# Prompt attention in four column groups of 32 keys, with transposes on VectorE and maxima gathered on GpSimd

## The reference

```python
scale = (D_NOPE + D_ROPE) ** -0.5
k_chunk = k_pos // CHUNK
def block(args):
    qb, pb = args
    s = jnp.einsum('bqhd,bkhd->bhqk', qb, k, preferred_element_type=F32) * scale
    mask = k_chunk[None, :] <= (pb // CHUNK)[:, None]
    p = jax.nn.softmax(jnp.where(mask[None, None], s, -jnp.inf), axis=-1)
    return jnp.einsum('bhqk,bkhd->bqhd', p.astype(v.dtype), v)
```

## Time and profile before

| what | us |
|---|---|
| median of 3 runs | 3896.78 (3894.89 to 3902.31) |
| the profiled execution, its own time | 3894.74 |
| its span, first to last instruction | 3893.0 |
| TensorE busy in the span | 3681.9 (95%) |
| VectorE, ScalarE busy | 1713.1 (44%), 1260.6 (32%) |
| GpSimd busy | 167.9 (4%) |
| the attention stage (first load to last store) | 1467.3 to 2128.9 |

### The profile page before, as it was taken

How to read it: one execution, slowest core, us unless ns; L and a number is a source line. 1 busy time by engine, 2 the same in 40 slices (tenths; PEclk the granted TensorE clock), 3 DMA queues, 4 the chain that set the end, 5 groups by cost and what they waited for, 6 DMA issues and landing times. The chain is left out here.

```text
span 3893.0 us, 64007 instructions
## 1 busy us (share of the span) xinstructions
PE 3681.9 (95%) x25552; PEld 2615.4 (67%) x25552; DVE 1713.1 (44%) x4404; ACT 1260.6 (32%) x3117; POOL 167.9 (4%) x193
## 2 busy tenths in 40 slices
PE   6999999979998888999999998999999999899998
PEld 3777777758887545666665445677767767677775
DVE  2443434445554244655555222221121122499996
ACT  1111111125553225655554001222122111355553
POOL 0000000011110000000000000000000000000100
PEclk8999999989999998999999999999999999899999
DMA  7111111143210011000002664111111111434433
GB/s 289 48 52 60 46 46 46 44 110 109 79 53 28 21 50 36 24 22 17 12 14 77 214 219 141 71 65 59 70 61 57 70 70 65 179 114 149 153 129 117
DMA packets 123523, 319.68 MB, mean 82 GB/s; under 512 B 38744, under 2 KB 57096, under 8 KB 118088
## 3 DMA queue, kind: packets, MB, share of 16 engines
q1 hardware_dynamic: 120568, 290.58, 20.5%
q0 software_dynamic: 2768, 26.47, 2.4%
HBM read 207.26 MB, written 109.74 MB: 81 GB/s over the span
## 5 line engine op out<-in xcount | busy, mean ns | idle before, releaser
L2373 PE MATMUL e_p<-e_hT,w_ahead 128*128 128x128 f32 x3264 | 410.7, 276 | 3.6 <-DMA shared<-w_in_o 3.6
L2373 PEld LDWEIGHTS e_p<-e_hT,w_ahead 128*128 128x128 f32 x3264 | 389.3, 193 | 11.7 <-issue 11.7
L535 PEld LDWEIGHTS a_p<-a_hT,w_even 128*128 128x128 f32 x3264 | 368.9, 193 | 9.4 <-issue 7.7
L535 PE MATMUL a_p<-a_hT,w_even 128*128 128x128 f32 x3264 | 369.1, 276 | 1.3 <-DVE a_hT L318 1.3
L550 PE MATMUL a_p<-w_even,a_hT 128*128 128x512 f32 (+2 forms) x1024 | 369.8, 522 | 0.0
L550 PEld LDWEIGHTS a_p<-w_even,a_hT 128*128 128x128 f32 x1024 | 193.9, 191 | 164.5 <-issue 115.4
L1696 DVE TENSOR_REDUCE q_mx<-q_sps 128x1 f32<-128x512 f32 (+4 forms) x320 | 181.5, 583 | 215.7 <-PE q_sps L1537 214.7
L2220 PE MATMUL c_b<-shared,c_oc 128*128 128x512 f32 x512 | 225.7, 601 | 11.6 <-DMA c_oc<-scr_ob 11.6
L2765 PE MATMUL h_b<-h_w,h_oT 128*128 128x512 f32 x512 | 236.6, 596 | 0.0
L2324 ACT ACTIVATE e_r<-e_p 128x512 f32<-128x512 f32 x66 | 39.4, 597 | 518.5 <-PE e_p L2379 299.0
L1625 ACT ACTIVATE q_P<-q_sps,q_mx 128x512 f32<-128x512 f32 (+4 forms) x320 | 190.7, 603 | 20.3 <-DVE q_mx L1701 15.5
(11 more groups left out here) (461 smaller groups left out, 5790.8 us busy)
## 6 DMA issues: line engine op xcount, KB each, us to landing
scr_qkg<-e_r SPq DMA_DIRECT2D x68, 512.0 KB, 2.6
h_rq<-scr_qkg SPq DMA_DIRECT2D x17, 2048.0 KB, 10.4
scr_iz<-e_r SPq DMA_DIRECT2D x34, 512.0 KB, 2.6
scr_qkv<-a_cv SPq DMA_DIRECT2D x17, 768.0 KB, 3.2
d_sc<-scr_qkv SPq DMA_DIRECT2D x17, 768.0 KB, 4.2
wa<-w_ada SPq DMA_DIRECT2D x8, 1536.0 KB, 16.2
w_ahead<-w_ada POOLq DMA_DIRECT2D x8, 1536.0 KB, 7.8
w_ahead<-w_in_o POOLq DMA_DIRECT2D x6, 2048.0 KB, 10.6
```

The costliest lines, as they stand in the source:

```text
L535: mm = pe.matmul(bank[g][:, (c % 4) * P:(c % 4 + 1) * P], w[:, k, c * P:(c + 1) * P], hT[:, p, k, :], start=k == 0, stop=k == KD - 1)
L2373: mm = pe.matmul(bank[n % 4][:, c * P:(c + 1) * P], w[k][:, a:a + P], hT[:, p, k, :], start=k == 0, stop=k == KD - 1)
```

## The change

The scores get another layout. A head's queries of one tile are cut in 4 blocks of 32 (`u`), and the keys of each tile in 4 groups of 32 (`i`). One matmul has 32 queries as stationary operand and all keys of one group (32·kt of them) as moving operand, and it writes the 32 partitions of column group `i`; so four matmuls fill 128 partitions, 16 make a head. In this layout a transpose within blocks of 32x32, which VectorE has as an instruction (`dve.transpose`, shown as STREAM_TRANSPOSE), gives just what the values' product needs, in SBUF. TensorE's transposes and both engines' copies out of PSUM go away.

A query's keys now lie on four partitions. VectorE writes four partial (negated) maxima, GpSimd copies three of them to the first 32 partitions, VectorE takes the least, and GpSimd copies that to the other three groups of partitions. The row sums are added over the groups by a matmul with `fold` (`sums`). The mask becomes a 97th row of the contraction: a row of keys that holds -1e30 for unseen keys, which GpSimd sets in `keys` and clears tile by tile (`unmask`), against ones in the queries.

The work goes by parts of a head: a tile with kt up to 8 has one part per head (4 blocks of queries), the others have two (2 blocks each). A part takes one of three slots of two PSUM banks. That makes 64 + 128 = 192 parts. TensorE writes the scores of a part and then a share of the products of the pair two before; all auxiliary matmuls use one bank, `aux`, half by half.

The functions before stand above; these are the new lines that the prediction speaks of:

```diff
+            for half in kT:
+                hidden = half[HQ:HQ + 1, :, :].rearrange("p h (t c) -> p h t c", c=P)
+                pool.memset(hidden[:, :, :, 0:CH], 0.0)
+                pool.memset(hidden[:, :, :, CH:P], UNSEEN)
...
+    PAIRS, PARTS, B, SLOTS, HELD = HB // 2, 4, 32, 3, 4
...
+        Pr = sb(f"{tag}_P", [P, 2, PARTS, 512])
+        PT = sb(f"{tag}_PT", [P, 4, NT, P])
+        low = sb(f"{tag}_low", [P, HELD, PARTS, PARTS])
+        top = sb(f"{tag}_top", [P, HELD, PARTS])
+        ls = sb(f"{tag}_ls", [P, 2, PARTS, HB])
...
+        sps = ps(f"{tag}_sps", [P, 2 * SLOTS, 512])
+        aux, ops = ps(f"{tag}_aux"), ps(f"{tag}_o")
...
+                self.kt = m + 1
+                self.n = B * self.kt
+                self.wide = 128 if self.kt <= 4 else 256 if self.kt <= 8 else 512
+                self.own = 4 if self.kt <= 8 else 2
+                self.parts = PARTS // self.own
+                self.s0 = prev.s0 + HB * prev.parts if prev else 0
...
+            pool.memset(qT[HQ:HQ + 1, :, :, 0:CH], 1.0)
+            pool.memset(qT[HQ:HQ + 1, :, :, CH:P], 0.0).then_inc(ones, 1)
+            def unmask(m, half):
+                pool.wait_ge(sc_r, sizes[m].exps(4 * half + 3))
+                pool.memset(kT[half][HQ:HQ + 1, :, m * P + CH:(m + 1) * P], 0.0).then_inc(seen, 1)
+            for s, (z, h, part) in enumerate(parts_in_order):
+                if part == 0 and h == 4 and after(z):
+                    unmask(z.m, 0)
+                if part == 0 and h == 0 and z.m:
+                    unmask(z.m - 1, 1)
+                pool.wait_ge(part_r, s + 1)
+                for i in range(1, 4):
+                    u = pool.tensor_copy(low[0:B, s % HELD, i, 0:z.own], low[i * B:(i + 1) * B, s % HELD, 0, 0:z.own])
+                u.then_inc(gathered, 1)
+                pool.wait_ge(low_r, s + 1)
+                for i in range(1, 4):
+                    u = pool.tensor_copy(top[i * B:(i + 1) * B, s % HELD, 0:z.own], top[0:B, s % HELD, 0:z.own])
+                u.then_inc(top_r, 1)
...
+            def scores(z, h, part):
+                if part == 0:
+                    pe.wait_ge(qT_out, 2 * z.m + 1 + h // 4)
+                    if h == 0:
+                        since(pe, seen, 2 * z.m - 1)
+                        pe.wait_ge(ones, 1)
+                    if h == 4:
+                        since(pe, seen, 2 * z.m)
+                keys = kT[h // 4][0:HQ + 1, h % 4, :].rearrange("p (t c) -> p t c", c=P)[:, 0:z.kt, :]
+                since(pe, exp_r, z.slot(h, part) - SLOTS + 1)
+                to = z.scores_of(h, part)
+                for u in range(z.own):
+                    at = (part * z.own + u) * B
+                    for i in range(4):
+                        mm = pe.matmul(to[i * B:(i + 1) * B, u, :].rearrange("p (t c) -> p t c", c=B), qT[0:HQ + 1, z.m % 2, h, at:at + B],
+                                       keys[:, :, i * B:(i + 1) * B], start=True, stop=True)
+                mm.then_inc(sc_r, 1)
...
+            def products(z, j, n, of):
+                if n == 0:
+                    pe.wait_ge(pt_r, no(z, 2 * j) + 2)
+                    since(pe, oU_r, z.m * PAIRS + j)
+                mm = None
+                for c in range(z.kt * n // of, z.kt * (n + 1) // of):
                     for p in range(2):
...
+                        mm = pe.matmul(ops[p * DV:(p + 1) * DV, 0:P], V[:, c, 2 * j + p, :], PT[:, (2 * j + p) % 4, c, :], start=c == 0, stop=c == z.kt - 1)
+                if n == of - 1:
                     mm.then_inc(pv_r, 1)
             def pair(z, j):
...
+                a, b = ahead(z, 2 * j, 2), ahead(z, 2 * j, 3)
+                steps = [(*g, part) for g in (a, b) if g for part in range(g[0].parts)]
+                before = (z, j - 1) if j else (sizes[z.m - 1], PAIRS - 1) if z.m else None
+                middle = len(steps) // 2
...
+                for i, step in enumerate(steps):
+                    if i == middle:
+                        if j == 0 and z.m:
+                            sums(z.m - 1)
+                        if j == 1 and after(z):
+                            queries(z.m + 1, 0)
+                        if j == 2 and after(z):
+                            queries_T(z.m + 1, 0)
+                    scores(*step)
+                    if before:
+                        products(*before, i, len(steps))
+                if before and not steps:
+                    products(*before, 0, 1)
...
+            def exps(z, h, part):
+                n, s = no(z, h), z.slot(h, part)
+                act.wait_ge(top_r, s + 1)
+                since(act, pt_r, n - 1)
+                if h == 0 and part == 0:
+                    since(act, folded, z.m - 1)
+                of = z.scores_of(h, part)
+                for u in range(z.own):
+                    at = part * z.own + u
+                    a = act.activation(Pr[:, n % 2, at, 0:z.n], of[:, u, :], ACT.Exp, bias=top[:, s % HELD, u:u + 1],
+                                       accum_out=ls[:, z.m % 2, at, h:h + 1])
                 a.then_inc(exp_r, 1)
...
+            def maxima(z, h, part):
+                s = z.slot(h, part)
+                dve.wait_ge(sc_r, s + 1)
+                dve.tensor_reduce(low[:, s % HELD, 0, 0:z.own], z.scores_of(h, part), AX, ALU.max, negate=True).then_inc(part_r, 1)
+            def lowest(z, h, part):
+                s = z.slot(h, part)
+                dve.wait_ge(gathered, s + 1)
+                since(dve, exp_r, s - HELD + 1)
+                dve.tensor_reduce(top[0:B, s % HELD, 0:z.own], low[0:B, s % HELD, :, 0:z.own].rearrange("p i u -> p u i"), AX, ALU.min).then_inc(low_r, 1)
+            def turned(z, h, part):
+                n = no(z, h)
+                if part == 0:
+                    since(dve, pv_r, n // 2 - 1)
+                to = PT[:, n % 4, 0:z.kt, :].rearrange("p t (u q) -> p u t q", q=B)
+                dve.wait_ge(exp_r, z.slot(h, part) + 1)
+                own = slice(part * z.own, (part + 1) * z.own)
+                u = dve.transpose(to[:, own], Pr[:, n % 2, own, 0:z.n].rearrange("p u (t k) -> p u t k", k=B))
+                if part == z.parts - 1:
+                    u.then_inc(pt_r, 1)
...
+            for s in range(2):
+                maxima(*parts_in_order[s])
+                lowest(*parts_in_order[s])
+            for s, (z, h, part) in enumerate(parts_in_order):
+                if h == 2 and part == 0 and z.m:
+                    gates(z.m - 1)
+                if h == 5 and part == 0 and z.m:
+                    gated(z.m - 1)
+                following = parts_in_order[s + 2] if s + 2 < len(parts_in_order) else None
+                if following:
+                    maxima(*following)
+                turned(z, h, part)
+                if following:
+                    lowest(*following)
```

More of the change, by code:

```diff
@@ L1583, in pair @@
[L1583 to L1596 removed]
+                if j == 3 and after(z):
+                    queries_T(z.m + 1, 1)
@@ L1597, in _ @@
+            pe.wait_ge(wu_in, 3 * 16)
+            latents(0)
+            queries(0, 1)
+            queries(0, 0)
+            queries_T(0, 0)
+            queries_T(0, 1)
+            pe.wait_ge(init, 1)
+            for h in range(2):
+                for part in range(sizes[0].parts):
+                    scores(sizes[0], h, part)
             for z in sizes:
```

336 lines of the change are left out of this document (112 added, 224 removed).

## The result

The changed kernel takes 3886.49 us (median of 15 executions, 3882.19 to 3896.92), the kernel before 3896.73 in the same comparison (15 executions); the ratio is 0.9979, 95% interval 0.997 to 0.9988. So it is 10 us faster, where 69 were forecast. The profiled execution's span is 3887.0, 6.0 less than before. In it the attention stage runs from its first load at 1470.63 to 2122.9, 652.3 us against 661.6, so it is 9.3 us shorter. The other 3.4 us lie ahead of it: this execution reached the stage that much later.

A forecast was written before the change was run, and what follows sets the result against it. The prediction took TensorE's own work to bound the attention stage. TensorE's work, waits, start and end summed to 592.5 us against 661.6, −69 us, so 3828 us; 8-in-10 range 3755 to 3985, by its own terms 3790 to 3875.

The forecast's parts named there:

- TensorE's work: Attention stage: TensorE's sum 516 us, 90 less than before; large tiles 2.6·kt + 11.2 each, small ones 2.6·kt + 8.8.
- 3 (pairs only): Rival for the scores: column groups run only in pairs, +233 us, 4060 us; chance 0.07.
- 4 (free changes): Rival for TensorE: changes between groups of 32 and 64 columns cost nothing, −57 us, 3771 us; chance 0.08.
- The upper half of short passes: Scores at small kt: very short passes may not issue fast enough, 0 to 13 us; 6 us taken.
- the mask's cover: Mask rows in `keys`: four GpSimd memsets, about 15 us, taken as hidden while TensorE still makes values of `keys`.
- Rival 2: VectorE's transpose runs at half rate: stage 645 us, time 3880 us; chance 0.12.
- Rival 1: GpSimd is the bound: at 0.55 us per tiny copy 3980 us, forecast lost from 0.42; chance 0.17.
- two waits are real: Small tiles: TensorE waits for the reciprocal and the rotation, together 0.32·kt + 2.7 us per tile.
- TensorE's PEclk 1.00 from the third tile on: Sign expected in the next profile: TensorE at full clock from the attention stage's third tile on.
- The end: After the last scores: maximum, spread, exponentials, transpose, last products (counted elsewhere) and gates, 10 us.
- allowance of 1.5 us a tile: Large tiles: 12 us in all for waits, because the tightest ring came near TensorE's work.
- a ring that doesn't bind: Large tiles, four parts' chain from scores through maxima, GpSimd and exponentials: 12.1 us at kt = 16 against TensorE's 13.2.

The follow-up runs named there:

- e6_pt5: e5 with room for five instead of four heads of transposed probabilities: 3782.09 us, ratio 0.9711.
- e7: The changed kernel with each of GpSimd's copies issued twice, the first three of each hop to a spare tile: 3985.07 us, ratio 1.0233.
- e1: The changed kernel with ScalarE's copies of queries (0) and queries_T (0) ahead of its copy of the finished products: 3862.23 us, ratio 0.9914.
- e2: The changed kernel with VectorE's reciprocal, gates, rotation and gated outputs placed earlier, in the small tiles alone: 3839.51 us, ratio 0.9857.
- e4: The changed kernel with the orders of e1 and e2, and ScalarE copying the next tile's latents ahead of exponentials: 3824.93 us, ratio 0.9816.
- e5: e4 with ScalarE's copies of queries (0) and the first queries_T ahead of the pair's first head's exponentials, in small tiles: 3798.66 us, ratio 0.9749.
- e3: The changed kernel with TensorE's five waits in tiles of 2 to 8 key tiles filled with unused transposes, nothing moved: 3856.11 us, ratio 0.99.
- e11: The changed kernel with VectorE instead of GpSimd gathering the partial maxima and spreading the least, in the small tiles: 3923.82 us, ratio 1.0082.

## Why the prediction was wrong

Its stage was 592.5 us; 652.3 were measured, 59.8 more: start −2.3 (15.2 against 17.5), small tiles +59.1 (262.1 against 203), large tiles −3.3 (358.7 against 362), end +6.3. The 3886 lie within the range of 8 in 10, but that was wide for rivals of which none came true; by its own terms (waits none or double among them) the forecast reached up to 3875 only. The table compares tile by tile, from a tile's first scores to the next one's (us, worked out from the starts in the traces; the prediction's are 2.92·kt + 11.5 and 2.6·kt + 12.7):

| kt | predicted | measured | e6_pt5 | without the predicted waits |
|---|---|---|---|---|
| 2 | 17.3 | 27.1 | 19.8 | 14.0 |
| 3 | 20.3 | 31.4 | 19.7 | 16.6 |
| 5 | 26.1 | 35.3 | 22.7 | 21.8 |
| 8 | 34.9 | 41.1 | 29.3 | 29.6 |
| 9 | 36.1 | 37.5 | 34.5 | 34.6 |
| 12 | 43.9 | 44.4 | 41.8 | 42.4 |
| 15 | 51.7 | 51.9 | 49.6 | 50.2 |

- **TensorE's work: right.** With the waits taken out (e6_pt5, last columns) tiles of 5 and more come within 0.9 us of 2.6·kt + 8.8 and 2.6·kt + 11.2. The first four do not: 11.2 of the 13.4 us of waits that are left in the small tiles are theirs, and the clock is 0.71 and 0.74 at kt = 1 and 2. The four column groups run beside each other (16 passes of 512 columns in 1.71 us), a change between 32 and 64 columns costs 0.15, as the one between 64 and 128 did. Of my rivals, 3 (pairs only) and 4 (free changes) are thereby out. The rule of "TensorEngine Tiling (Array Packing)" in the Trainium skill, Key Properties, that changing the mode drains TensorE, holds for this change too. The trace has 0.29 for two.
- **The upper half of short passes: too high.** At kt = 1 in e6_pt5, scores and the products behind them start 0.39 us apart, of which 0.21 are columns (32 passes of 32 in eight rounds of 0.027) and 0.15 the change. The 6 us of this term aren't there.
- **VectorE's transpose and GpSimd's copies: right**, 1.23 us against 1.2 and 0.18 to 0.20 against 0.2. So was the mask's cover: its four memsets of 3.51 us run from 1423.0 to 1436.9 inside `keys`, which from its load of `q_wu` to the first load of attention takes 49.3 us as before. Rival 2 (half rate) is out. Rival 1's condition, 0.42 per copy, didn't arise, but its mechanism was put wrongly: e7 shows that copies as slow as 0.4 already cost 99 us, not because GpSimd becomes the bound (it is busy for 424 of 716 us) but through the latency of each part.
- **The failed step: "In small tiles there is one part per head, and two waits are real."** There are five. I had found those behind VectorE's reciprocal and rotation, and given them 0.32·kt + 2.7 a tile, 33 us. I had followed neither ScalarE's queue (its copies out of `aux` stand behind exponentials and behind `weighted`) nor the fact that `aux` is one bank for seven users, so that each of them waits for the reader of the one before. TensorE's idle time is 61.9 us: 29 more. The two that I had priced were right in size, 34.4 us (8.9 for the reciprocal, 25.5 for rotation and gated output). The three that I had not come to 24.2: `sums` 10.8, `gates_T` 5.9, the second `queries_T` 7.5. e1, e2, e4 and e5 take these waits away by order alone, and the small tiles go from 262.1 to 181.8 us.
- **The second half of it: "TensorE's PEclk 1.00 from the third tile on".** I priced no lower clock. It is 0.81 granted on average up to kt = 8. e3 gives it back without touching a wait: 28.6 us. As an estimate from these rows, 29 of waits and 29 to 38 of clock (0.19 of 262.1 is 50 us of clock, of which TensorE's busy share, 200.24/262.1, is 38), less 6 of short passes, make up the 59; the two overlap, so the split is good to some 10 us. The same matmuls are busy for 168.6 us in e6_pt5 at a clock of 0.94, 31.6 less.
- **The end: 16.3 instead of 10.** TensorE issues the products of the last two pairs behind all scores, 64 passes each, 3.71 and 5.10 us in the trace (at full clock, in e2_dve, both take 3.71). I had counted them in the last tile. So the last tile is short of its sum by 7.2 us (47.1 against 54.3), the end is over by 6.3, and the tiles of 9 to 15 are over by 4.4 (311.7 against 307.3).
- **The large tiles' allowance of 1.5 us a tile, 12 in all: about right in size, wrong in cause.** I attributed it to a ring that doesn't bind. TensorE's idle time there is 18.5 us in the changed kernel, of which 12.9 are the same waits ahead of auxiliary matmuls as in the small tiles and 5.5 waits ahead of scores. With the former taken away by order (e1, e4, e5) 11 us stand ahead of scores. They come from the buffer of four heads, whose wait I had described ahead of the ring without pricing it; with room for five (e6) the large tiles are 13.4 us shorter and 0.3 us of waits are left.

The signs of being wrong that I had set (VectorE waiting for GpSimd, TensorE for exponentials) would not have caught this: in the small tiles the one comes to 11.9 us and the other to 1.5.

The direction was right, the size wasn't: 69 us were forecast for 10. That the sign came out right is a difference of two large numbers, 64 us won in the large tiles and 54 to 57 lost in the small ones. e4_all, at 3824.93, reaches the forecast's 3828 with nothing but places in two orders moved. That the two agree is chance in part, since its large tiles take 351.6 us where the forecast had 362.

## What to carry to other kernels

When a matmul stream is made shorter, list for every auxiliary matmul who frees its buffer and what stands ahead of that reader in its own queue; with a single shared bank each user inherits the slowest reader, and small tiles show it first, because the stream between two users shrinks and the readers' work doesn't. Price a wait of TensorE twice, once for itself and once for what runs at the lower clock behind it; filling it with unused transposes is a cheap test of the second price. And before removing an engine's share of work, try the order: e2's moved lines gave 47 us, and moving work to the "nearer" engine (e11) cost 37.

## What the runs showed of the hardware

- TensorE's lower clock cost 28.6 of 262 us in a stretch whose single waits were no longer than 3.4 us (clock 0.81 granted); 406 unused transposes in these waits brought it to 0.95 and made the stretch shorter (e3_idle).
- Four column groups of 32 run at four times one's rate in float32: 16 passes of 512 columns in 1.71 us, worked out of a period of 2.87; for passes of 32 columns (e6_pt5, kt = 1) scores and change together take 0.39 us, 0.03 more than columns and change make.
- A change between groups of 32 and 64 columns costs 0.15 us (two in 0.29 of the same period).
- VectorE transposes blocks of 32x32 in the time that its maximum takes for as many elements: 1.23 us for 1024 elements and 0.83 for 640, the maximum 1.21 to 1.23 and 0.81 to 0.83.
- A copy of 32 partitions by 2 or 4 elements takes 0.18 to 0.20 us on GpSimd and 0.16 on VectorE: at this size the choice between them is one of queues.
